# Feed-forward in two phases: gate and up units first, then the output chunks one by one

## The reference, cut to what matters

```python
for l in range(DEPTH):                                   # 2
    x = x + 0.5 * swiglu(rmsnorm(x, g_ffn1[l]), w_ffn1_gate[l], w_ffn1_up[l], w_ffn1_down[l])
    u = rmsnorm(x, g_mix[l])
    ...                                                  # three branches of u, gated and merged
    x = x + merged @ w_out[l]
    x = x + 0.5 * swiglu(rmsnorm(x, g_ffn2[l]), w_ffn2_gate[l], w_ffn2_up[l], w_ffn2_down[l])

def swiglu(h, w_gate, w_up, w_down):                     # 1024 -> 2816 -> 1024
    return (jax.nn.silu(h @ w_gate) * (h @ w_up)) @ w_down
```

## Time and profile before

| | |
|---|---|
| median of 3 runs | 2681.4 us (2679.96 to 2682.03) |
| span of the profiled execution | 2678.4 us |
| PE busy | 2580.5 us (96%) |
| DVE busy | 1507.2 us (56%) |
| ACT busy | 899.9 us (34%) |
| mean granted TensorE clock | 0.984 |
| HBM traffic over the span | 263 GB/s |

### The profile page before, as it was taken

The page is one execution under the profiler, slowest core; times in us unless marked ns, Lnnn a source line. Parts: engine busy times, 40 slices in busy tenths (PEclk is TensorE's granted clock), DMA queues, the critical chain, the costliest instruction groups (busy, mean ns, idle before and its releaser), DMA issues.

```text
span 2678.4 us, 47640 instructions
## 1 busy us (share of the span) xinstructions
PE 2580.5 (96%) x19446; PEld 2091.0 (78%) x19447; DVE 1507.2 (56%) x2697; ACT 899.9 (34%) x1400; POOL 36.6 (1%) x24
## 2 busy tenths in 40 slices
PE   7999999999999999999999988999999999999998
PEld 6999699999999969999988878955555555555554
DVE  5666666666766666666676776534434434434344
ACT  4344454443444445443454544411111111111111
POOL 0000000000000000000000110000000000000000
PEclk9999999999999989999999998999999999999999
DMA  9644544454444445544454224689999999999997
GB/s 267 235 180 165 205 179 181 166 188 176 166 178 185 165 191 221 189 164 175 180 188 165 95 101 162 267 333 426 430 430 430 430 430 430 430 430 430 430 430 299
DMA packets 70926, 704.62 MB, mean 263 GB/s; under 512 B 11063, under 2 KB 11319, under 8 KB 14343
## 3 DMA queue, kind: packets, MB, share of 16 engines
q1 hardware_dynamic: 65736, 695.11, 64.8%
q0 software_dynamic: 5088, 8.05, 1.4%
HBM read 699.43 MB, written 3.67 MB: 263 GB/s over the span
## 4 chain that ended last, share of the span: by engine, by line
PE 76%; DMA 13%; DVE 6%; ACT 3%; issue 1%; SPq 0%; DVEq 0%; ACTq 0%
PE ps L1662 15%; PE ps L1665 15%; PE ps L1666 15%; DMA slot<-in_experts 13%; PE ps L2175 9%; PE ps L2199 5%; PE ps L2155 5%; PE ps L2212 2%; DVE u_lo L1002 2%; PE ps L1693 1%; PE ps L1696 1%; PE ps L1697 1%; PE ps L2185 1%; ACT u_hi L562 1%; ACT hs L585 1%
## 5 line engine op out<-in xcount | busy, mean ns | idle before, releaser
L1002 DVE TENSOR_TENSOR u_lo<-ring,u_hi 128x1024 fp32r<-128x1024 f32 x500 | 615.7, 1237 | 446.8 <-ACT u_hi L562 444.0
L562 ACT ACTIVATE u_hi<-ring 128x1024 fp32r<-128x1024 f32 x498 | 524.1, 1057 | 684.7 <-PE ps L1662 640.1
L1662 PE MATMUL ps<-hs,u_hi 128*128 128x256 f32 x2408 | 693.8, 288 | 18.4 <-DVE hs L1028 17.3
L1665 PE MATMUL ps<-hs,u_hi 128*128 128x256 f32 x2408 | 686.8, 285 | 0.0
L1666 PE MATMUL ps<-hs,u_lo 128*128 128x256 f32 x2408 | 686.4, 285 | 0.0
L1662 PEld LDWEIGHTS ps<-hs,u_hi 128*128 128x128 f32 x2408 | 467.7, 194 | 30.1 <-issue 19.6
L1665 PEld LDWEIGHTS ps<-hs,u_hi 128*128 128x128 f32 x2408 | 468.0, 194 | 0.4
L1666 PEld LDWEIGHTS ps<-hs,u_lo 128*128 128x128 f32 x2408 | 467.5, 194 | 0.0
L2175 PE MATMUL ps<-slot,xg 128*64 128x256 f32 x4032 | 461.0, 380 | 6.2 <-DMA slot<-in_experts 6.2
L2175 PEld LDWEIGHTS ps<-slot,xg 128*64 128x64 f32 x4032 | 287.7, 137 | 211.7 <-issue 66.3
L2199 PE MATMUL ps<-slot,eact 128*64 128x512 f32 x1008 | 244.2, 605 | 0.0
(11 more groups left out here) (368 smaller groups left out, 3027.5 us busy)
## 6 DMA issues: line engine op xcount, KB each, us to landing
slot<-in_experts SPq DMA_DIRECT2D x248, 1536.0 KB, 18.8
ring<-in_stream SPq DMA_DIRECT2D x184, 1536.0 KB, 6.4
extra_in<-in_experts SPq DMA_DIRECT2D x4, 1024.0 KB, 11.8
slot<-in_experts SPq DMA_DIRECT2D x4, 1024.0 KB, 4.9
bias<-bias_rows POOLq DMA_DIRECT2D x2, 1280.0 KB, 11.4
konst<-in_konst POOLq DMA_DIRECT2D x1, 2272.0 KB, 14.5
extra_out<-in_experts SPq DMA_DIRECT2D x4, 512.0 KB, 9.3
slot<-in_experts SPq DMA_DIRECT2D x4, 512.0 KB, 15.1
```

Of the source, the lines that this page charges most:

```text
L562: nc.scalar.activation(u_hi[buffer_of(l, k)][:, :], raw_unit(l, k), ACT.Copy).then_inc(unit_hi, 1)
L1002: nc.vector.tensor_tensor(u_lo[b][:, :], raw_unit(l, kk), u_hi[b][:, :].bitcast(F32), ALU.subtract).then_inc(unit_lo, 1)
L1662: mm = mm_(dst, hi, x_hi, start=first, stop=False, skip_group_check=True)
L1665: mm_(dst, hi, x_lo, start=False, stop=False, skip_group_check=True)
```

## The change

The order of a feed-forward's units becomes gate 0, up 0, gate 1, up 1, ... gate 21, up 21, and then 22 units of the down weights, laid out by output chunk: 22 blocks of 128 x 128 make one chunk, so chunks end within units 2, 5, 8, 10, 13, 16, 19 and 21 of the 22 (`DOWN_END`).

- `acts` holds all 22 tiles (11264 floats a partition in place of 2048), `gu` two slots, and gate and up of a tile go to two banks. PE waits for `gu_scaled` of tile i-2 before it writes tile i.
- The rounding of the hidden values moves from DVE (L1063) to ACT (`round_act`); the remainder on DVE moves behind the next unit's (`low_act`).
- PE runs 66 products in a row into one bank for each output chunk. DVE adds chunk m to `x` (`take_down`), ACT rounds it, DVE takes its remainder and adds up the squares pair by pair (`add_squares`), all written between the units of the chunks that follow. `h_ready`, `h_hi` and `x_ready` count chunks, no longer pairs.
- The output projection's eight chunks are treated in the same way (`take_out`).
- The larger `acts` covers `vecs`, from which the DMAs of `bias_rows` read. In the first feed-forward ACT waits for `rows_written` to reach all four DMAs, after hidden tile 3 and ahead of the loop over tiles 4 to 21.

```diff
-        gu = rest("gu", 4096, 4, 2, TOK)
-        acts = rest("acts", 6144, 4, 2, TOK, dt=F32R)
+        gu = rest("gu", 4096, 2, 2, TOK)
+        acts = rest("acts", 6144, FF_TILES * 2 * TOK, dt=F32R)
...
-        SSUM, DOWN = 2, 4
+        SSUM, FSUM, DOWN = 2, 6, 4
...
-            def round_x(q, gain):
-
-                for b in range(OUTS):
-                    a.wait_ge(x_ready, q * OUTS + (b + 1))
-                    for c in (2 * b, 2 * b + 1):
-                        op = nc.scalar.activation(hs[:, c, 0, :], x[:, c, :], ACT.Copy, scale=lp_all[:, q // 3, gain + c:gain + c + 1])
-                    op.then_inc(h_hi, 1)
-                    nc.scalar.activation(sq[:, 2 * b:2 * b + 2, :], x[:, 2 * b:2 * b + 2, :], ACT.Square).then_inc(sq_ready, 1)
...
+            def round_x(q, c, gain):
+
+                a.wait_ge(x_ready, q * DC + (c + 1))
+                nc.scalar.activation(hs[:, c, 0, :], x[:, c, :], ACT.Copy, scale=lp_all[:, q // 3, gain + c:gain + c + 1]).then_inc(h_hi, 1)
+                if c % 2:
+                    nc.scalar.activation(sq[:, c - 1:c + 1, :], x[:, c - 1:c + 1, :], ACT.Square).then_inc(sq_ready, 1)
...
+                def round_act(i, g=0):
+                    a.wait_ge(act_made, f_count(l, f, i, g))
+                    at = i * 2 * TOK if isinstance(g, int) else bass.ds(g * (12 * TOK) + i * 2 * TOK, TOK)
+                    dst = acts[:, at:at + TOK] if isinstance(g, int) else acts[:, at]
+                    nc.scalar.activation(dst, gu[:, i % 2, 1, :], ACT.Copy).then_inc(act_rounded, 1)
+
+                def pair(i, g=0):
+                    round_unit(l, k0 + 2 * i + 5, g)
+                    silu_of(i, g)
+                    round_unit(l, k0 + 2 * i + 6, g)
+                    round_act(i, g)
...
+                if l == 0 and f == 0:
+                    a.wait_ge(rows_written, 4 * 16)
+                with a.Fori(0, (FF_TILES - 4) // 6) as g:
+                    for i in range(4, 10):
+                        pair(i, g)
+                for u in range(2, FF_TILES):
+                    if u < FF_TILES - 1:
+                        round_unit(l, k0 + DOWN0 + u + 3)
+                    else:
+                        next_unit(l, k0 + DOWN0 + u + 3)
+                    if gain is not None and u - 1 in DOWN_END:
+                        round_x(q + 1, DOWN_END.index(u - 1), gain)
+                if gain is not None:
+                    round_x(q + 1, DC - 1, gain)
...
+                def pair(i, g=0):
+                    scale_of(i, g)
+                    low_unit(l, k0 + 2 * i + 5, g)
+                    act_of(i, g)
+                    low_unit(l, k0 + 2 * i + 6, g)
+                    low_act(i, g)
...
+                def take_down(m):
+                    v.wait_ge(down_done, (l * 2 + f) * DC + m + 1)
+                    nc.vector.scalar_tensor_tensor(out=x[:, m, :], in0=ps[:, DOWN + m % 4, 0:TOK], scalar=0.5, in1=x[:, m, :],
+                                                   op0=ALU.mult, op1=ALU.add).then_inc(x_ready, 1)
+
+                for u in range(2, FF_TILES):
+                    low_unit(l, k0 + DOWN0 + u + 3)
+                    if u in DOWN_END:
+                        take_down(DOWN_END.index(u))
+                    if gain is not None and u - 2 in DOWN_END:
+                        low_x(q + 1, DOWN_END.index(u - 2), gain)
+                if gain is not None:
+                    low_x(q + 1, DC - 1, gain)
...
+                for m in range(DC - 2, DC):
+                    take_out(m)
+                    low_x(l * 3 + 2, m - 1, LP_FFN2)
+                low_x(l * 3 + 2, DC - 1, LP_FFN2)
                 ffn(l, 1, LP_FFN1 if l + 1 < LAYERS else None)
...
+                    if i >= 2:
+                        pe.wait_ge(gu_scaled, f_count(l, f, i - 2, g))
```

More of the change, by code:

```diff
@@ L59 @@
 PASSES = TOK // CAP
-LAYER_STEPS, MOE_STEPS = 50, 2 * PAIRS + 1
+MOE_STEPS = 2 * PAIRS + 1
 ALPHA, LIMIT = 1.702, 7.0
 FFN1, QK0, V10, V20, G0, OUT0, FFN2 = 0, 66, 80, 88, 96, 133, 141
+DOWN0, FFN_UNITS = 2 * FF_TILES, 3 * FF_TILES
+DOWN_END = [(FF_TILES * (m + 1) - 1) // DC for m in range(DC)]
 LU = 207
@@ L640, in _ @@
                     a.wait_ge(par_landed, 16)
-                ffn(l, 0)
-                round_x(l * 3 + 1, LP_MIX)
+                    for c in range(DC):
+                        round_x(0, c, LP_FFN1)
+                ffn(l, 0, LP_MIX)
                 def take_proj(r):
@@ L1022, in scaled, with low_x @@
                                                       in1=rstd[:, 0:TOK], op0=ALU.mult, op1=ALU.mult)
-            def low_x(q, gain, b):
-                v.wait_ge(h_hi, q * OUTS + (b + 1))
-                for c in (2 * b, 2 * b + 1):
-                    op = nc.vector.scalar_tensor_tensor(out=hs[:, c, 1, :], in0=x[:, c, :], scalar=lp_all[:, q // 3, gain + c:gain + c + 1],
-                                                        in1=hs[:, c, 0, :].bitcast(F32), op0=ALU.mult, op1=ALU.subtract)
-                op.then_inc(h_ready, 1)
-            def update(add, q, gain):
-                for b in range(OUTS):
-                    add(b).then_inc(x_ready, 1)
-                    if gain is not None and b > 0:
-                        low_x(q, gain, b - 1)
-                if gain is not None:
-                    low_x(q, gain, OUTS - 1)
+            def low_x(q, c, gain):
+                v.wait_ge(h_hi, q * DC + (c + 1))
+                nc.vector.scalar_tensor_tensor(out=hs[:, c, 1, :], in0=x[:, c, :], scalar=lp_all[:, q // 3, gain + c:gain + c + 1],
+                                               in1=hs[:, c, 0, :].bitcast(F32), op0=ALU.mult, op1=ALU.subtract).then_inc(h_ready, 1)
+                if c in (3, 5):
+                    add_squares(q, c // 2)
             def modulate(known):
@@ L1720, in ffn, with up_gate @@
[L1720 to L1728 removed]
+                k0, q = (FFN1, FFN2)[f], l * 3 + 2 * f
+                def up_gate(i, g=0):
+                    bank = 2 * (i % 2)
+                    if i >= 2:
+                        pe.wait_ge(gu_scaled, f_count(l, f, i - 2, g))
+                    project(l, k0 + 2 * i, ps[:, bank, 0:TOK], hs, g, h_count=q * DC + 1 if i == 0 else None)
+                    project(l, k0 + 2 * i + 1, ps[:, bank + 1, 0:TOK], hs, g).then_inc(gu_ready, 1)
@@ new lines, in ffn @@
+                up_gate(0)
+                sum_partitions(q, FSUM)
+                for i in range(1, 4):
+                    up_gate(i)
+                with pe.Fori(0, (FF_TILES - 4) // 6) as g:
+                    for i in range(4, 10):
+                        up_gate(i, g)
+                for m in range(DC):
+                    if m >= 4:
+                        pe.wait_ge(x_ready, (q + 1) * DC + m - 3)
+                    for i in range(FF_TILES):
+                        n = m * FF_TILES + i
+                        k = k0 + DOWN0 + n // DC
+                        if n % DC == 0:
+                            pe.wait_ge(unit_lo, unit_count(l, k))
+                        if m == 0:
+                            pe.wait_ge(act_ready, f_count(l, f, i))
+                        b, w = layer_buffer(k), slice(n % DC * P, (n % DC + 1) * P)
+                        high, low = acts[:, i * 2 * TOK:i * 2 * TOK + TOK], acts[:, i * 2 * TOK + TOK:(i + 1) * 2 * TOK]
+                        mm = products(ps[:, DOWN + m % 4, 0:TOK], u_hi[b][:, w], u_lo[b][:, w], high, low, i == 0, i == FF_TILES - 1,
+                                      begin=n % DC == 0)
+                    mm.then_inc(down_done, 1)
@@ L2368, in ffn_units @@
 def ffn_units(gate, up, down):
[L2369 to L2373 removed]
+    pairs = np.stack([units_of(by_output(gate)), units_of(by_output(up))], 1)
+    return np.concatenate([pairs.reshape(-1, P, UNIT), units_of(by_output(down))])
 def tiles_of(units):
```

180 lines of the change are left out of this document (68 added, 112 removed).

## The result

| | before | after |
|---|---|---|
| median of 7 runs | 2681.07 us (2679.76 to 2682.03) | 2674.77 us (2671.14 to 2677.21) |
| span of the profiled execution | 2678.4 us | 2672.8 us |
| mean granted TensorE clock | 0.984 | 0.981 |

The ratio is 0.9975, with a 95% interval of 0.9964 to 0.9986: 6.3 us less where 9.2 were forecast. The forecast called it faster, and 2674.77 lies in its own range of 2666 to 2677.

What follows compares the result with a forecast made beforehand. Three quarters of the span hang on PE, 13% on the experts' weight DMAs. Gains of 15.6 + 4.0 + 1.3 = 20.9 us less 11.7 lost made 9.2 us, so 2681.4 becomes 2672 us (own range 2666 to 2677).

Steps and rivals of the forecast that it cites:

- Part 1: Ends of three feed-forwards with a norm behind: chunk 7's chain and the squares are hidden; gain 5.2 us each, 15.6 us.
- rival 3: Joints do not close: chunk 7's chain or squares leave 1.4 us more at each of five; 2679 us, chance 0.14.
- the sum's own matmul: End of a feed-forward: the matmul of the sum over squares stays exposed, about 0.5 us of the 5.7 lost.
- Part 2: Output projection, two places: DVE is behind, PE idles some 1.8 and 1.4 us; gain 2.0 us each, 4.0 us.
- DVE's list: Output projection's end: DVE's queued additions, remainders and squares, with chunk 6 ready near 499.8 us and chunk 7 near 500.3.
- Part 3: Last feed-forward: the 0.77 us wait for the last hidden tile goes, squares start earlier (0.5); gain 1.3 us.
- Part 4: Inside the phases: DVE's and ACT's work fits in each hidden tile's 5.76 us of PE; cost nothing.
- Rival 4: Small engines slip inside phase one: each of 88 hidden tiles 0.1 us late, 8.8 us lost; 2681 us, chance 0.08.
- Part 5: First feed-forward: ACT halts for the bias-row writes, landing at 72 us; PE idles 9.9 us; loss 11.7 us with clock dip.
- The clock's share: After PE's idle gap in the first feed-forward: a clock dip costing 1.8 us at worst.
- Rival 1: Bias-row write keeps its own pace, landing at 89.2 us; loss 28.9 us against 20.9 gained; 2689 us, chance 0.14.
- the start's: Program start: per-chunk rounding saves 0.8 us, kept only if the new wait causes no idle.

Runs made afterwards that it cites:

- i_heads: The changed kernel, wait kept, with each of the ten rows of vecs written by a DMA of its own; 2705.09 us, ratio 1.0092.
- g_floor: The changed kernel with ACT's wait for rows_written moved ahead of the fourth unit's rounding, so ahead of nearly all weights; 2701.42 us, ratio 1.008.

## Why the prediction was right, and where it was not

- **Part 1, ends of feed-forwards: right.** 5.2 each were forecast. The count of 250 "minus some 5" starts came out as 251 and 252, and the ledger gives 5.8 and 5.6. So rival 3, by which the joints do not close, is out. The half microsecond charged for the sum's own matmul was too much. Behind the last unit DVE works as worked out: an addition of 0.42 at 234.81 and remainders of 0.48 and 0.49, done at 236.3, while PE runs on without a gap.
- **Part 2, output projection: right in mechanism, undersized.** 2.0 each were forecast, 3.2 measured by undoing it. Two idles were forecast, of 1.8 and 1.4; they are 0.8 and 0.9, from 490 to 520 us:

```profile
PE ps L1686 <- DVE sqsum L1039: 0.9, 1, 0.9
PE ps L1690 <- DVE hs L1052: 0.8, 1, 0.8
```

  The step that failed is the length of DVE's list. Its order was right, and so nearly was its begin: 0.2 us behind the start of the stage by forecast, and with it as measured (the first product over the new `hs` is at 507.74, the list begins at 507.75). But an addition and a remainder follow their forerunners after 0.33 to 0.4 us where their shown lengths of 0.41 and 0.48 were summed: chunk 6 is ready at 510.8, 3.1 us into the stage, where the prediction had 3.8. In the same way the squares end at 515.9, 8.1 us into the stage, where it had 9.0.
- **Part 3, the last feed-forward: right**, 1.0 against 1.3.
- **Part 4, inside the phases: right.** PE never waits for `gu_scaled` or for hidden values; between 720 and 880 us it starts 1336 products as in the earlier trace rows; and with the rounding back on DVE the layers take as long. Rival 4 is out.
- **Part 5, the new wait: right in kind, undersized by 5.4 us.** 11.7 were forecast; 17.3 measured by the ledger, 16.8 by taking it away. The clock's share was right (2.0 against 1.8). The term that was off is the landing, 77.3 where 72 was taken. The steps behind it were "the little that is left drips while weights pass" and "from there q0 is alone", with 1.9 to 8 us of work left. A wait 11.5 us earlier in PE's work brought the landing 2 us forward; with one refill in all it still took 51.7 us. So the pace of the rows was mostly the write's own: their last packet ends between 73.4 and 79.5 us in all the kernels that write them so, whatever the weights do. Something does drip while weights pass, but it is the tiny packets behind the rows, some 10 us of them before and under 2 with the weights halted. The falling traffic in the earlier trace rows is both: the last rows, slow by themselves, to 78.9 us, and then the tail. That the landing came within the bounds of 64 to 81 was in part luck.
- **The skill's rule on turns** (the Trainium skill, "DMA: Bandwidth & Descriptors", section on queues, rings and completion order): by it a quiet weight queue leaves the whole engine to q0. The tail of tiny packets fits it, which is no proof (114 in 9 us beside weights, 70 in 1.3 us without); for the rows themselves the rule is no help, since q0, with no other queue beside it, used 60.3% of the engines and moved 79 GB/s. **Rival 1**, the write's own pace, was thus nearer to the cause than its chance of 0.14 said, but wrong in its price: the weights do cost the write some 16 us, 12 of them already saved by the changed kernel's wait, so it landed at 77.3 and not at 89.2.
- **A sign of being wrong that came up.** The prediction named waits for the remainders of the next input above 5 us in total. They are 5.1. Of these 3.5 are one wait at the start of the program, where the kernel before has 4.3 and which is no joint; at the joints 1.6 are left.
- **The sum.** The parts give 25.4 us of gain without the wait (20.9 forecast, 21.7 with the start's), and 16.8 to 17.3 of loss (11.7 forecast). Two errors of about 5 us on opposite sides left 8.6 against 9.2 at the end of the layers; that the sum came out so near is luck. The time itself moved by 6.3.
- **The gap between 8.6 and 6.3.** The profile of after has the long second block, 3.9 us more than before's, which comes and goes by itself and which no part of the prediction had. The seven times of after lie at 2671.1 to 2671.6 (three) and 2674.8 to 2677.2 (four), a gap of that size, and the median falls into the upper group. That the upper group are the runs with the long block is likely, but shown for the profiled one (2674.77) alone.
- **Open:** what the packets of 8 bytes behind the rows are, and what lowers the clock in the second block of some executions.

## What to carry to other kernels

Where a stage ends in eight outputs at once and the next starts from all of them, finishing them one by one pays twice: the order alone returned half of each joint's 5.7 us here, and the small work written between the units that follow the other half. When a buffer grows over one that a DMA still reads, find out first what sets that DMA's pace, by a run in which it is alone; a landing time that merely coincides with busy neighbours says nothing of what happens when they stop. And where a row of SBUF has to be repeated many times in HBM, try writing it once and repeating it from there: here that took 12.3 us in place of more than 50.

## What the runs showed of the hardware that was not expected

- DMAs that each read 2 KB of one SBUF partition 128 times moved about 27 GB/s (i_heads, 40 to 50 us), even with 93.1% of the 16 engines' time on them. Four DMAs of two to four such rows moved 79 GB/s on 60.3% of it, and 28 GB/s on 27.4% at their end (g_floor). The same rows repeated from HBM moved at 213 GB/s beside the weights. That the partition's reads are what bounds it is a reading that fits these runs; no run measured it by itself.
- The landing of such a write came some 10 us after its last packet of data where weights passed beside it, and under 2 us after it where they had been halted.
- Such a DMA costs others more than its bytes: with 93.1% of the engines' time on it a weight tile lands in 40.6 us (median), with the rows from HBM in 8.1.
- The landings that the profile lists for several DMAs on one semaphore can be too early: 13 us for three writes of 0.5 MB each, when most of their bytes moved after 35 us.
- After 15.1 us of idle time PE started again at the lower of its two clock levels (a granted 0.79 from 76 to 96 us), and lost 2.0 us by it; after 26.5 us of idle time on the kernel before it lost 1.6.
